# Both projections of a second transformer block, with queries and keys built token by token

## The reference

```python
# layer A: x -> q, k, v, gate, forget logits
q, k, v, gate, f_logit = split(rmsnorm(h, norm_a_g) @ w_in_a)        # 16 heads of 64
q = rmsnorm(q.reshape(b, s, 16, 64), qnorm_a_g); k = rmsnorm(k..., knorm_a_g)
o = fox_attention(q, k, v, log_sigmoid(f_logit + b_forget))
h = h + (o * silu(gate)) @ w_out_a
# layer B
k_s, v_s = split(rmsnorm(h, kv_norm_g) @ w_kv)                        # 4 heads of 64 each
k = partial_rope(rmsnorm(k_s, knorm_b_g), positions); v = v_s
q, gate = split(rmsnorm(h, norm_b_g) @ w_in_b)                        # 16 heads of 64
q = partial_rope(rmsnorm(q, qnorm_b_g), positions)
o = swa_sink_attention(q, k, v, sinks)
h = h + (o * silu(gate)) @ w_out_b
```

## Time and profile before

| | us |
|---|---|
| median of 3 runs (3036.03 to 3040.45) | 3037.71 |
| the profiled execution | 3037.1 |
| its span, first to last instruction | 3035.3 |
| TensorE busy | 2561.3 (84%) |
| VectorE busy | 1866.0 (61%) |
| ScalarE busy | 1349.5 (44%) |
| GpSimd busy | 828.9 (27%) |

### The profile page before, as it was taken

How to read it: one execution, slowest core, us unless ns; L and a number is a source line. 1 busy time by engine, 2 the same in 40 slices (tenths; PEclk the granted TensorE clock), 3 DMA queues, 4 the chain that set the end, 5 groups by cost and what they waited for, 6 DMA issues and landing times. The chain is left out here.

```text
span 3035.3 us, 37631 instructions
## 1 busy us (share of the span) xinstructions
PE 2561.3 (84%) x13397; PEld 2025.7 (67%) x13397; DVE 1866.0 (61%) x2549; ACT 1349.5 (44%) x2313; POOL 828.9 (27%) x649
## 2 busy tenths in 40 slices
PE   1999799999768999999708989988885969878969
PEld 1786389787667888888507867766554756656547
DVE  5663555786338999999563299614444546852981
ACT  2353144784217888888443222225654132222540
POOL 0121012212003111111130033317776004531950
PEclk9999899999859999999859999989998979989989
DMA  5541000002039999999470011230003110013201
GB/s 213 170 153 28 0 1 1 1 29 84 30 139 413 405 414 409 415 419 411 162 276 22 21 35 43 62 132 29 29 29 118 42 56 28 28 46 123 96 8 49
DMA packets 144318, 392.35 MB, mean 129 GB/s; under 512 B 11835, under 2 KB 89760, under 8 KB 131762
## 3 DMA queue, kind: packets, MB, share of 16 engines
q1 hardware_dynamic: 131070, 345.69, 30.2%
q0 software_dynamic: 12096, 43.06, 3.5%
q10 hardware_dynamic: 1012, 1.72, 0.2%
HBM read 344.24 MB, written 46.20 MB: 129 GB/s over the span
## 5 line engine op out<-in xcount | busy, mean ns | idle before, releaser
L2435 POOL TENSOR_SCALAR fox_l<-fox_l,stat 128x256 f32<-128x256 f32 (+7 forms) x128 | 219.0, 1726 | 76.4 <-DVE stat L2471 76.4
L2463 DVE CUSTOM_DVE_ANT_0 fox_l<-PS,fox_c 128x256 f32<-128x256 f32 (+7 forms) x128 | 92.1, 756 | 155.3 <-PE PS L2517 110.0
L328 PE MATMUL PS<-uTh,wah 128*128 128x512 f32 x400 | 170.4, 426 | 0.0
L329 PE MATMUL PS<-uTl,wah 128*128 128x512 f32 x400 | 157.0, 393 | 0.0
L330 PE MATMUL PS<-uTh,wa_rest 128*128 128x512 f32 x400 | 156.8, 392 | 0.0
L2424 ACT ACTIVATE fox_l<-fox_l,stat 128x256 f32<-128x256 f32 (+7 forms) x128 | 98.4, 770 | 75.1 <-DVE stat L2463 75.1
L328 PE MATMUL PS<-xTh,wbh 128*128 128x512 f32 x288 | 121.4, 421 | 0.0
L2167 POOL TENSOR_SCALAR a_y<-a_corr 128x512 f32<-128x512 f32 x32 | 40.0, 1249 | 289.7 <-DVEq L2312 289.7
L2993 POOL TENSOR_SCALAR win_p<-win_p,stat 128x256 f32<-128x256 f32 (+1 forms) x128 | 110.7, 888 | 20.0 <-DVE stat L3044 20.0
L2299 DVE RECIPROCAL a_y<-a_y 128x512 f32<-128x512 f32 x32 | 107.2, 3349 | 10.0 <-ACT a_y L2227 9.8
L329 PE MATMUL PS<-xTl,wbh 128*128 128x512 f32 x288 | 112.6, 391 | 0.0
(11 more groups left out here) (529 smaller groups left out, 7896.2 us busy)
## 6 DMA issues: line engine op xcount, KB each, us to landing
we0g<-in_w_expert_gate SPq DMA_DIRECT2D x16, 2048.0 KB, 11.1
we0u<-in_w_expert_up SPq DMA_DIRECT2D x16, 2048.0 KB
we1g<-in_w_expert_gate SPq DMA_DIRECT2D x16, 2048.0 KB, 11.0
we0d<-in_w_expert_down SPq DMA_DIRECT2D x16, 2048.0 KB
we1u<-in_w_expert_up SPq DMA_DIRECT2D x16, 2048.0 KB
we1d<-in_w_expert_down SPq DMA_DIRECT2D x16, 2048.0 KB
wada_rest<-in_w_ada SPq DMA_DIRECT2D x16, 1024.0 KB, 5.2
wa<-in_w_in_a SPq DMA_DIRECT2D x25, 512.0 KB, 4.1
```

Of the source, the lines that this page charges most:

```text
L328: nc.tensor.matmul(out, lh, rh, start=start, stop=False)
L329: nc.tensor.matmul(out, lh, rl, start=False, stop=False)
L2435: nc.gpsimd.tensor_scalar(prob(p, e)[:, 0:K], prob(p, e)[:, 0:K], rsum[:, u % 8:u % 8 + 1], None, ALU.mult).then_inc(p_ready, 1)
L2463: nc.vector.tensor_tensor_reduce(out=prob(p, e)[:, 0:K], in0=PS[:, 2 * e:2 * e + 2, :].rearrange("p a b -> p (a b)")[:, 0:K], in1=C[:, h % ...
```

## The change

Both projections now make queries and keys with **tokens on partitions**: a unit is 128 tokens by 512 columns (8 heads). The weights come as groups of 512 columns (2 MB each, `wqk`, `wq`, `wkv`) in place of chunks of 128. Layer A has the same 32 units for q and k; layer B makes k and v together in 8 units of 512 columns (the first 256 are k, the rest v) and q in 16, so 24 units pass through the chain. Per unit:

- ScalarE squares the unit from bank to bank; VectorE sums each head's 64 squares by a reduction to 128x8 (128x4 for k); ScalarE takes the root of 128x8; VectorE makes reciprocal and correction in five steps on 128x8, then one 128x512 product into one of two buffers (`pad`, called `qn` in the phases). No column sums on TensorE, no GpSimd.
- In layer B VectorE then turns 8 pairs a head in place: four products on 128x64 (gains and cosines or sines folded into a table of 8 columns a tile) and two sums. k is written twice, for the two halves of partitions that attention wants.
- TensorE transposes the buffer back, four float32 instructions of 128x128 into banks 5 to 7 (`turn`), and ScalarE evacuates with the head gain as scale (`evacuate`).
- TensorE's queue is unit u, then `turn(u - 1)`, which waits for the chain of u-1; unit u waits for the chain of u-3.

v of layer A goes through four staging buffers into DRAM and comes back into `va` during the gate units, since its place holds weights meanwhile. The trigonometry shrinks to 128x64 and the position load to 1024 single numbers. The barrier behind the clearing of semaphores goes, and a clearing is added at the start of `phase_fox`.

```diff
+    NU, NG = 4 * T, 2 * KD
...
+            sp.dma_start(wf[:, :, :], chunk_of(w, slice(3 * D, 3 * D + P))).then_inc(wf_in, 16)
+            group(0)
+            for u in range(2 * T):
+                i, t = u // T, u % T
+                sp.wait_ge(v_out, u + 1)
+                sp.dma_start(env.v_dram[t * P:(t + 1) * P, i * HALF:(i + 1) * HALF], stage[:, u % 4, :]
+                             ).then_inc(v_saved[u % 4], 16)
...
+            sp.wait_ge(f_mm, 2)
+            group(1)
+            for i in range(2, 4):
+                sp.wait_ge(mm, T * (i - 1))
+                group(i)
+            sp.wait_ge(mm, 3 * T)
+            for c in range(3):
+                gate_chunk(c)
+            sp.wait_ge(mm, 4 * T)
+            for t in range(T):
+                sp.dma_start(env.va[:, t, :], env.v_dram[t * P:(t + 1) * P, :]).then_inc(va_in, 16)
...
+            def evacuate(u):
+                i, t = u // T, u % T
+                act.wait_ge(t_ready, u + 1)
+                if u == 2 * T:
+                    act.wait_ge(c_saved, 16)
+                nc.scalar.activation(dst[i][:, 4 * (i % 2):4 * (i % 2) + 4, t * P:(t + 1) * P],
+                                     PS[:, 5 + u % 3, :].rearrange("p (c s) -> p c s", s=P), ACT.Copy,
+                                     scale=col(env, gains[i])).then_inc(t_out, 1)
...
+            for u in range(NU):
+                i, t = u // T, u % T
+                act.wait_ge(mm, u + 1)
+                if u >= 2:
+                    act.wait_ge(sums, u - 1)
+                nc.scalar.activation(PS[:, 3 + u % 2, :], PS[:, u % 3, :], ACT.Square).then_inc(squares, 1)
                 if u >= 1:
...
+                    evacuate(u - 1)
+                act.wait_ge(sums, u + 1)
+                if u >= 2:
+                    act.wait_ge(normed, u - 1)
+                nc.scalar.activation(stats(1, u), stats(0, u), ACT.Sqrt, bias=env.eps[:, 0:1], scale=1.0 / HD
+                                     ).then_inc(root, 1)
+                if i < 3 and 2 <= t < 6:
+                    group_hi(i + 1, t - 2)
+                elif i == 3 and t in (2, 4, 6):
+                    gate_hi(t // 2 - 1)
+            evacuate(NU - 1)
             for g in range(NG):
...
+            for u in range(NU):
+                i, t = u // T, u % T
+                ss, rs, nw = stats(0, u), stats(1, u), stats(2, u)
+                dve.wait_ge(squares, u + 1)
+                nc.vector.tensor_reduce(ss, heads(PS[:, 3 + u % 2, :]), AX_X, ALU.add).then_inc(sums, 1)
+                dve.wait_ge(root, u + 1)
+                do(nc.vector.reciprocal(rs, rs))
+                do(nc.vector.tensor_tensor(nw, rs, rs, ALU.mult))
+                do(nc.vector.scalar_tensor_tensor(nw, ss, EPS * HD, nw, ALU.add, ALU.mult))
+                do(nc.vector.tensor_scalar(nw, nw, -0.5 / HD, 1.5, ALU.mult, ALU.add))
+                do(nc.vector.tensor_tensor(rs, rs, nw, ALU.mult))
+                if u >= 2:
+                    dve.wait_ge(t_ready, u - 1)
+                nc.vector.tensor_tensor(heads(qn[u % 2][:, :]), heads(PS[:, u % 3, :]),
+                                        rs.unsqueeze(2).to_broadcast([P, GH, HD]), ALU.mult).then_inc(normed, 1)
                 if u % 2 == 0 and u < 14:
                     forget(u // 2)
...
+            def turn(u):
+                pe.wait_ge(normed, u + 1)
+                if u >= 3:
+                    pe.wait_ge(t_out, u - 2)
+                elif u >= 1:
+                    pe.wait_ge(f_act, 1)
+                for c in range(4):
+                    last = nc.tensor.transpose(PS[:, 5 + u % 3, c * P:(c + 1) * P], qn[u % 2][:, c * P:(c + 1) * P],
+                                               env.ident)
+                last.then_inc(t_ready, 1)
 
             for u in range(NU):
-                pe.wait_ge(wl_done, 2 + u // 2)
-                if u >= 4:
-                    pe.wait_ge(normed, u - 3)
+                i, t = u // T, u % T
+                tt = slice(t * P, (t + 1) * P)
+                if u >= 3:
+                    pe.wait_ge(normed, u - 2)
                 else:
                     pe.wait_ge(v_out, 2 * T - 3 + u)
-                chunk_product(u % 4, 1 + u // 2, u % 2).then_inc(mm, 1)
+                for k in range(KD):
+                    if t == 0 and k % 2 == 0:
+                        pe.wait_ge(wg_lo, 4 * i + k // 2 + 1)
+                    last = split_product(nc, PS[:, u % 3, :], (uh[:, k, tt], ul[:, k, tt]),
+                                         (wgh[i % 2][:, k, :], wgl[i % 2][:, k, :]), k == 0, k == KD - 1)
+                last.then_inc(mm, 1)
                 if u >= 1:
-                    head_sums(u - 1)
+                    turn(u - 1)
...
+        dve.wait_ge(pos_in, 48)
+        do(nc.vector.tensor_copy(pos_f[:, :], pos[:, :]))
+        for i in range(8):
+            last = nc.vector.tensor_scalar(ang[:, :, i], pos_f[:, :], float(inv[i]), None, ALU.mult)
+        do(last)
...
+        for i in range(2):
+            first, second = (gr[:, i, 8 * j:8 * j + 8].unsqueeze(1).to_broadcast([P, T, 8]) for j in range(2))
+            for at, (trig, g) in enumerate(((cos, first), (sin, second), (cos, second), (sin, first))):
+                last = nc.vector.tensor_tensor(env.rope_tab[:, i, at, :, :], trig, g, ALU.mult)
...
+    NU, NG = 3 * T, 2 * KD
...
+                if i == 0:
+                    for to in range(2):
+                        last = nc.vector.tensor_tensor(x[:, to::2, :], src, r, ALU.mult)
+                else:
+                    last = nc.vector.tensor_tensor(x, src, r, ALU.mult)
+                last.then_inc(scaled, 1)
+                dve.wait_ge(scaled, u + 1)
+                a, b = x[:, :, 0:8], x[:, :, 8:16]
+                tab = [env.rope_tab[:, 1 if i == 0 else 0, at, t, :].unsqueeze(1).to_broadcast([P, 8, 8])
+                       for at in range(4)]
+                for at, half in enumerate((a, b, b, a)):
+                    last = nc.vector.tensor_tensor(rt[:, at, :, :], half, tab[at], ALU.mult)
+                do(last)
+                nc.vector.tensor_tensor(a, rt[:, 0, :, :], rt[:, 1, :, :], ALU.subtract)
+                nc.vector.tensor_tensor(b, rt[:, 2, :, :], rt[:, 3, :, :], ALU.add).then_inc(roped, 1)
...
-    nc.clear_and_free_semaphores(taken)
-    nc.all_engine_barrier()
+    env.spent = taken[:]
+    del taken[:]
     phase_combine(nc, A, env, sem)
-    second_block(nc, A, env, sem, out)
```

More of the change, by code:

```diff
@@ L177, in setup @@
     env.csil = m.fixed("csil", [P, KD])
+    env.pad = [m.fixed(f"pad{i}", [P, HALF]) for i in range(2)]
 def col(env, name, k=0):
@@ L2132, in phase_a_projection @@
[L2132 to L2149 removed]
+    wf_in, wf_hi, wf_lo, f_mm = sem("wf_in"), sem("wf_hi"), sem("wf_lo"), sem("f_mm")
@@ L2313, in _ @@
-            for c in range(4 + NU // 2, NCH):
-                chunk_lo(c)
+                if i < 3 and 2 <= t < 6:
+                    group_lo(i + 1, t - 2)
+                elif i == 3 and t in (2, 4, 6):
+                    gate_lo(t // 2 - 1)
+            for c in range(3, KD):
+                gate_lo(c)
         @block.tensor
@@ L2729, in phase_b_projection @@
+    mm, squares, sums, root, scaled, roped = (sem("b_mm"), sem("b_squares"), sem("b_sums"), sem("b_root"),
+                                              sem("b_scaled"), sem("b_roped"))
+    v_out, t_ready, t_out, dve_step = sem("bv_out"), sem("b_t"), sem("b_t_out"), sem("b_dve")
     silu, g_saved = sem("bg_silu"), [sem("bg_saved0"), sem("bg_saved1")]
-    units = ([("k", c, n) for c in range(2) for n in range(2)] + [("q", c, n) for c in range(KD) for n in range(2)])
-    NU, NG = len(units), 2 * KD
+    NU, NG = 3 * T, 2 * KD
```

599 lines of the change are left out of this document (289 added, 310 removed).

## The result

The changed kernel takes **2932 us** (median of four runs, 2931.2 to 2934.1) against 3038.6 for the one before: a ratio of 0.965, with a 95% interval from 0.964 to 0.967, or 106 us gained where 82.5 were forecast. The profiled execution has a span of 2929.0 us against 3035.3. The direction and the places are as forecast; 2932 lies 8 us under the range.

A forecast was written before the change was run, and what follows sets the result against it. The prediction took the ring of sums, root, reciprocal and GpSimd product, VectorE in its middle, as the bound. Gains of 16 in A, 65 in B and 1.2 elsewhere, 82.5 with rounding, gave 2955 us, range 2940 to 2985.

The forecast's parts named there:

- The bound: Both projections before: the sums, root, reciprocal, GpSimd product ring limits them, VectorE in its middle; its reciprocal takes 3.35 us a unit.
- TensorE's cost per unit: Both projections: each unit's group of four float32 transposes, with the change of operands around it, costs 0.91 us.
- the cheap end: Both projections: lower price for four float32 transposes, 0.43 us, from a burst at 0.107 each.
- the range's low end: Whole kernel: 2940 us, with the scan's wait hidden (5 us) and a transpose group at 0.71 us (11 us).
- The chain: From a unit's products' end: 3.75 us to `normed` in A, 4.85 to `roped` in B, in time by 2.6 and 1.5.
- The wait in A: Near A's fifth unit: the forget scan's reciprocal makes TensorE wait 3.0 us, then some 2 us at the low clock.
- B's start: Layer B's projection: three VectorE steps of 1.23 precede the first matmul, 3.7 us; the first unit takes 7.7 us.
- Elsewhere: Outside the projections: removing the barrier gains 1.2 us; new clearing costs nothing; position load, possibly 0 to 3 us, taken as nothing.
- Dear transposes: Rival, both projections: four transposes cost 0.69 us, adding 14.6 us over 56 units, about 2970; chance 0.10.
- Late chain: Rival, layer B: small VectorE steps of 0.5 us make an 8.2 us chain, 22 us more, 2980 to 2990; chance 0.10.
- the prediction's rule of every second unit: Layer B: a late transpose group delays the next products too, so only every second unit waits, 12 x 1.8 = 22 us.
- Low clock: Rival, both projections: chain past 9.2 us makes each unit's products 5.44 us dearer, up to 305 us, some 3260; chance 0.03.

The follow-up runs named there:

- twelve steps: Twelve more dependent VectorE steps on 128x8 in layer B's chain, put into the changed kernel ahead of the last two rope steps: 2964.4 us.
- 24 steps: Twenty-four more dependent VectorE steps on 128x8 in layer B's chain, put into the changed kernel ahead of the last two rope steps: 3029.3 us.

## Why the prediction was off, step by step

- **The bound: right in A, half said in B.** Without the reciprocal A's window fell to 204.7 (forecast 203.2 and a little); in B a third of the loss stayed, with GpSimd's product named at each wait. That a weight's low part takes VectorE 2.20 us beside GpSimd and 1.23 without it held: it is 1.22 in B now.
- **TensorE's cost per unit: the step that failed.** The term 0.91 for the group was the sums' whole cost carried over to other instructions, on the reading that half of it was a change of operands and that a float32 matmul of 512 columns is two passes of 0.227 us. That matmul takes 0.86 us itself, the change 0.05, and the group measured 0.47. By terms: A 32 x 0.44 = 14.1 us (forecast gain 16, measured 30.3), B 24 x 0.44 = 10.6 (65, measured 75.3). The row that gives it stood in the prediction's own text as the cheap end, 4 x 0.107 = 0.43; the change of operands was added to it without a row. So the range's low end, which still had 0.71 for the group, did not reach the cheap end of its own bounds: with 0.43 + 0.05 it would have stood near 2926.
- **The chain: right.** 3.6 and 4.67 us against 3.75 and 4.85. Due was not 6.35 but 5.91, as the group ahead is shorter; the slack in B was 1.2 us and not 1.5, and still enough.
- **The wait in A: right in place, and in size partly by luck,** 3.35 + 1.7 for 3.0 + 2.0. With the true 5.91 us a unit the forecast's own terms give 15.6 - 11.8 = 3.8; VectorE's steps came some 0.3 shorter. The first transposes, forecast to wait 0.3, started 0.2 late (1722.02, 0.40 behind the last product in place of 0.23).
- **B's start: right.** 3.6 us from 2445.70 to the first matmul at 2449.32 (forecast 3.7). From there to the gate's end 231.7 us were measured; the forecast's 7.7 + 125.1 + 21.8 + 87.0 with 0.47 in place of 0.91 gives 231.1. The first unit, from 2449.32, took 8.3 us where 7.7 were forecast, which is the rest.
- **Elsewhere:** layer A starts its v 0.6 us sooner relative to the start of the kernel, where 1.2 were expected; since that start lies anywhere in 6.8 us among traces of the same code, what the barrier was worth is not shown. Attention and output stages are unchanged to 0.3 us between the two traces, so no cost of the position load is seen.
- **Rivals.** Dear transposes: the opposite held. The Trainium skill, "TensorE: Matmul & The Clock Gate", Part 4, has some 275 ns for a transpose in a kernel; here four cost 0.47 us, 118 ns each, and the granted clock over 94.4 us of units that each hold four of them was 1.00. Whether transposes alone would keep the clock up no run here shows: the longest row of them, 32 in 5.48 us, stands behind a wait of 5.39 us. Late chain: did not occur; where it was forced by twelve steps, it cost 32 us, where the prediction's rule of every second unit gives 17, or 28 with the allowance for weights. Low clock: its price was wrong by far. The prediction took it that every wait of 2.8 us or more is followed by a whole unit at the low clock. The 2.8 stands in none of its rows; the trace before has a wait of 2.83 us with low clock behind it and one of 2.60 without, and with 24 steps the low clock came behind waits from 1.87 us on, stayed away behind one of 3.26, and lasted 2 to 5 us.

## What to carry over

A price for a new instruction is taken from a row of that instruction, even a short burst elsewhere, and not from what stood in the same slot before; an overhead that is inferred as a difference should be looked for where two such instructions follow each other directly. For a chain behind a pipelined unit ask two things: does it end before its result is due, and how long is the longest ring through all in-order queues, one engine's own work per unit among them, for once the chain is late every unit pays that ring. A long step on an engine with slack costs the engine that has none its length less the slack, and here 1.7 us of low clock behind it; cut in pieces and spread it cost nothing.

## What the runs showed of the hardware

- A float32 matmul took 0.86 us for 512 columns and 0.44 for 256, 4 cycles a column at the full clock, and is recorded as two instructions; the float32 transpose 0.107 us for 128 columns, 2 cycles; the same data movement as an ordinary float32 matmul with the identity costs twice as much (0.92 against 0.47 us for four).
- Going over from one sort of matmul to another and back costs 0.04 to 0.05 us, not 0.46.
- After waits of up to 1.2 us the clock stayed full. After 18 of the 21 waits from 1.76 to 3.57 us in the run with 24 steps it was low for 2 to 5 us, and then full again, wait after wait; after the other three, of 1.76, 1.99 and 3.26 us, it stayed full, as it did after one of 2.56 us in the run with ordinary matmuls. The low clock cost time (1.7 us) only where TensorE was itself the bound.
- VectorE steps on 128x8 stay 0.20 us apart in a row of twelve dependent ones: 2.37 us.
